# A two-block transformer kernel on one core: the first mixer's projections on rows that are not yet normed

## The reference

```
n = rmsnorm(h, g_mix)            # h * rsqrt(mean(h*h) + 1e-6) * g_mix
proj = n @ w_in                  # queries, 3 pairs of keys and values, gates, and 3 inputs of a convolution
y_conv = short_conv_mixer(b_gate, c_gate, h_conv, conv_w, w_conv_out)   # (b_gate * conv(c_gate * h_conv)) @ w_conv_out
k_cmp = compress(k_c, cmp_pos_k, w1, w2)   # blocks of 32 rows + position, then gelu(blk @ w1) @ w2; the same for v_cmp
o_all = nsa_attention(q, k_cmp, v_cmp, k_s, v_s, k_w, v_w)
mix = sigmoid(g_conv) * y_conv + sigmoid(g_attn) * (gated sum of o_all) @ w_attn_out
h = h + mix @ w_o
```

## Time and profile before

| | |
|---|---|
| time, median of 3 runs | 747.07 us (746.95 to 748.43) |
| the profiled execution's own time | 746.89 us |
| its span, first to last instruction | 745.2 us |
| PE busy | 740.4 us (99%) |
| weight loads on PE busy | 641.4 us (86%) |
| DVE busy | 518.0 us (70%) |
| ACT busy | 416.4 us (56%) |
| POOL busy | 66.5 us (9%) |
| DMA queue of SP: share of the 16 engines | 52.6% |

### The profile page before, as it was taken

One profiled execution on the slowest core, in us unless ns is written; L12 is line 12 of the kernel. 1 busy time (PEld: TensorE's weight loads), 2 busy tenths in 40 slices (PEclk: granted clock), 3 DMA queues, 4 the chain that ended last, 5 costly groups with the idle time before them and its releaser, 6 DMA issues.

```text
span 745.2 us, 11582 instructions
## 1 busy us (share of the span) xinstructions
PE 740.4 (99%) x4563; PEld 641.4 (86%) x4563; DVE 518.0 (70%) x834; ACT 416.4 (56%) x788; POOL 66.5 (9%) x103
## 2 busy tenths in 40 slices
PE   9999999999999999999999999999999999999998
PEld 8999999877888888888888888887888888888886
DVE  5784677885756678887367757898667777447762
ACT  5575557556463455565356546597646656345640
POOL 6300000000010000430000004400100000000000
PEclk9999999999999999999999999999999999999999
DMA  8998444343455546766656461735355655656611
GB/s 266 297 311 274 85 109 153 114 128 123 146 170 197 167 152 222 198 213 228 188 172 212 171 226 54 251 124 174 111 168 170 191 204 174 222 170 188 207 57 56
DMA packets 99209, 131.26 MB, mean 176 GB/s; under 512 B 5357, under 2 KB 79163, under 8 KB 99156
## 3 DMA queue, kind: packets, MB, share of 16 engines
q1 hardware_dynamic: 96564, 125.58, 52.6%
q0 software_dynamic: 2304, 4.43, 2.7%
q10 hardware_dynamic: 288, 0.52, 0.2%
HBM read 128.68 MB, written 1.84 MB: 175 GB/s over the span
## 4 chain that ended last, share of the span: by engine, by line
PE 97%; DVE 2%; ACT 1%; issue 0%; POOL 0%; POOLq 0%
PE B L1626 39%; PE B L1592 22%; PE B L1597 11%; PE B L1581 11%; PE B L1805 2%; PE B L1852 2%; PE B L1815 2%; PE B L1639 1%; PE B L1685 1%; PE B L1633 1%; DVE LO L1002 1%; PE B L1808 1%; PE B L1832 1%; PE B L1730 1%; PE B L1791 0%; PE B L1729 0%
## 5 line engine op out<-in xcount | busy, mean ns | idle before, releaser
L1002 DVE TENSOR_TENSOR LO<-RAW,HI 128x1024 fp32r<-128x1024 f32 x236 | 282.5, 1236 | 101.0 <-ACT HI L538 100.5
L1626 PE MATMUL B<-HI,AA 128*128 128x512 f32 (+1 forms) x960 | 286.8, 376 | 0.3 <-DVE AA L1008 0.2
L538 ACT ACTIVATE HI<-RAW 128x1024 fp32r<-128x1024 f32 (+1 forms) x240 | 237.2, 1038 | 63.1 <-PE B L1626 58.2
L1626 PEld LDWEIGHTS B<-HI,AA 128*128 128x128 f32 x960 | 175.7, 188 | 33.8 <-issue 1.6
L1592 PE MATMUL B<-AA,HI 128*128 128x512 f32 x704 | 179.2, 393 | 0.0
L1626 PE MATMUL B<-LO,AA 128*128 128x512 f32 (+1 forms) x480 | 178.6, 372 | 0.0
L1592 PEld LDWEIGHTS B<-AA,HI 128*128 128x128 f32 x704 | 126.8, 189 | 23.0 <-issue 0.7
L1626 PEld LDWEIGHTS B<-LO,AA 128*128 128x128 f32 x480 | 90.6, 189 | 14.6
L1597 PEld LDWEIGHTS B<-AA,LO 128*128 128x128 f32 x704 | 96.6, 190 | 7.1
L1597 PE MATMUL B<-AA,LO 128*128 128x256 f32 x704 | 98.8, 282 | 0.0
L1581 PE MATMUL B<-AA,HI 128*128 128x256 f32 x448 | 83.3, 287 | 0.0
(11 more groups left out here) (313 smaller groups left out, 634.9 us busy)
## 6 DMA issues: line engine op xcount, KB each, us to landing
RAW<-in_w_in SPq DMA_DIRECT2D x29, 1024.0 KB, 5.8
RAW<-in_w_gate SPq DMA_DIRECT2D x22, 1024.0 KB, 5.3
RAW<-in_w_up SPq DMA_DIRECT2D x22, 1024.0 KB, 5.3
RAW<-in_w_down SPq DMA_DIRECT2D x22, 1024.0 KB, 5.0
RAW<-in_w_in SPq DMA_DIRECT2D x10, 512.0 KB, 6.4
RAW<-in_w_attn_out SPq DMA_DIRECT2D x4, 1024.0 KB, 5.1
RAW<-in_w_o SPq DMA_DIRECT2D x4, 1024.0 KB, 5.0
RAW<-in_w_out SPq DMA_DIRECT2D x4, 1024.0 KB, 5.0
```

The lines of the kernel that those rows point to most:

```text
L538: e.activation(pieces(HI, NSPL, i, k), pieces(RAW, NRAW, i, k), ACT.Copy).then_inc(split_hi, 1)
L1002: e.tensor_tensor(pieces(LO, NSPL, i, k), pieces(RAW, NRAW, i, k), pieces(HI, NSPL, i, k), ALU.subtract).then_inc(split_lo, 1)
L1626: x = e.matmul(dst, a, w[:, t, c0:c0 + n], start=(first and t == 0 and k == 0), stop=(last and t == nk - 1 and k == 2))
```

## The change

The rows of x are turned as they land, with neither the norm's weights nor its factor. g_mix is loaded as 8 rows of 128, turned to one column for each group of 128 features (G8), and applied by DVE on the way out of PSUM into XT; ACT makes AH from XT, and DVE AL. The sums of squares follow later in the lists of ACT and DVE. The factor of each row is applied to what the first mixer's products give: over tokens on the free axis by a multiplication with RR (the factors spread over all partitions by a matmul with diagonals), over tokens on the partitions as a scale of the ACT instruction that reads the bank. The positions are no longer added to the blocks: they are two further columns (60 and 61, high part and rest) of the compression's stationary operand, and a new matrix SUMS1 adds them in the turn. The places of `root(1)` and of the loads into VR in POOL's list, and the weights' order, are not touched.

```diff
 SyncE
-                    e.dma_start(GAIN[0:128:64, :], A["g_mix"][0, :].rearrange("(a n) -> a n", a=2)).then_inc(row_in, 16)
+                    e.dma_start(GAIN, A["g_mix"][0, :].rearrange("(a n) -> a n", a=8)).then_inc(row_in, 16)
 GpSimd
             for kv in range(2):
                 e.memset(BLOCKS[kv][:, :, 0, 60:64].bitcast(F32), 0.0).then_inc(pads, 1)
+            e.memset(SUMS1, 1.0).then_inc(pads, 1)
+            for i, (base, sign) in enumerate(((-60, 1), (61, -1))):
+                e.wait_ge(pads, 5 + i)
+                e.affine_select(out=SUMS1, in_=SUMS1, compare_op=ALU.is_ge, fill=0.0, base=base, pattern=[[0, 64]],
+                                channel_multiplier=sign).then_inc(pads, 1)
+            e.wait_ge(pads, 7)
+            e.tensor_tensor(SUMS1, SUMS1, SUMS[:, :], ALU.add).then_inc(pads, 1)
...
             e.wait_ge(setup, FAR)
+            e.wait_ge(spread_sb, 1)
+            e.wait_ge(turn_lo, 4)
+            e.tensor_tensor(RR2, RR[:, :], RR[:, :], ALU.mult).then_inc(setup, 1)
+            def keys(br, c):
+                e.wait_ge(keys_act, 2 * br + c + 1)
+                e.tensor_tensor(KT[:, br, c, :], KT[:, br, c, :], RR[:, :], ALU.mult).then_inc(keys_sb, 1)
+            for c in range(2):
+                keys(0, c)
...
             e.wait_ge(setup, HMASK)
+            for u in range(4):
+                for k in range(2):
+                    e.wait_ge(q_act, 2 * u + k + 1)
+                    q = QT[:, u // 2, 2 * (u % 2) + k, :]
+                    e.tensor_tensor(q, q, RR[:, :], ALU.mult).then_inc(q_sb, 1)
             e.wait_ge(rel_sb, 1)
...
+            for c in range(2):
+                keys(1, c)
+            e.wait_ge(setup, SQUARED)
+            for i in range(2):
+                for c in range(2):
+                    e.wait_ge(cg_act, 2 * i + c + 1)
+                    e.tensor_tensor(CG[:, c, :], CG[:, c, :], RR2, ALU.mult).then_inc(cg_sb, 1)
+                for c in range(2):
+                    e.wait_ge(up_sb, 4 * i + 2 * c + 2)
+                    e.tensor_tensor(CG[:, c, :], CG[:, c, :], RR[:, :], ALU.mult).then_inc(cg_sb, 1)
 ScalarE
-            for t, h in ((0, 0), (1, 0), (0, 1)):
-                e.wait_ge(x_in[2 * t + h], 16)
-                squares(2 * t, X[:, t, :], QK[:, t, :], h)
+            def first_squares(h):
+                for t in range(2):
+                    e.wait_ge(x_in[2 * t + h], 16)
+                    squares(2 * t, X[:, t, :], QK[:, t, :], h)
+            def first_turned(n):
+                c, d = slice(4 * (n // 2), 4 * (n // 2) + 4), slice(128 * (n % 2), 128 * (n % 2) + 128)
+                e.wait_ge(scaled_sb, n + 1)
+                e.activation(AH[:, c, d], XT[:, c, d], ACT.Copy).then_inc(turn_hi, 1)
+            first_squares(0)
+            first_turned(0)
+            first_turned(1)
             hi(0, 0)
-            e.wait_ge(root_sb, 1)
...
+            first_turned(2)
+            first_turned(3)
             hi(0, 1)
-            for t in range(2):
-                turned(2 + t, B[5 + t], 4, t)
+            first_squares(1)
+            def spread(n):
+                e.wait_ge(spread_pe, n)
+                e.activation(RR[:, :], B[7][:, 0:S], ACT.Copy).then_inc(spread_sb, 1)
             hi(1)
+            spread(1)
+            e.wait_ge(rows_sb, 1)
+            e.wait_ge(pads, 4)
+            for kv in range(2):
+                e.activation(BLOCKS[kv][:, :, 0, 60], VT[:, 12 + 16 * kv:28 + 16 * kv], ACT.Copy).then_inc(block_hi, 1)
             def keys(br, c):
                 e.wait_ge(keys_pe, 2 * br + c + 1)
-                e.activation(KT[:, br, c, :], B[c][:, 0:S], ACT.Copy).then_inc(keys_sb, 1)
+                e.activation(KT[:, br, c, :], B[c][:, 0:S], ACT.Copy).then_inc(keys_act, 1)
...
             keys(0, 0)
 VectorE
             e.wait_ge(gain_pe, 1)
+            e.tensor_copy(G8, B[2][:, 0:8]).then_inc(half_sb, 1)
...
+            def gained(n):
+                c, d = first(n)
+                e.wait_ge(turn_pe, n + 1)
+                e.tensor_tensor(XT[:, c, d], B[5 + n % 2][:, :].rearrange("p (c q) -> p c q", c=4),
+                                G8[:, c].unsqueeze(2).to_broadcast([128, 4, 128]), ALU.mult).then_inc(scaled_sb, 1)
+            def first_low(n):
+                c, d = first(n)
+                e.wait_ge(turn_hi, n + 1)
+                e.tensor_tensor(AL[:, c, d], XT[:, c, d], AH[:, c, d], ALU.subtract).then_inc(turn_lo, 1)
...
+            gained(0)
+            gained(1)
+            first_low(0)
+            first_low(1)
+            lo(0, 0)
+            gained(2)
+            gained(3)
+            first_low(2)
+            first_low(3)
+            lo(0, 1)
             e.wait_ge(squares_sb, 4)
             e.scalar_tensor_tensor(ST[:, 4:6], ST[:, 0:4:2], EPS, ST[:, 1:4:2], ALU.add, ALU.add).then_inc(mean_sb, 1)
...
+            lo(1, 0)
+            e.wait_ge(setup, IDENT)
             e.wait_ge(root_sb, 1)
...
+            diagonals(ST[:, 6:8])
+            e.tensor_scalar(ST[:, 14:16], ST[:, 6:8], 0.5, None, ALU.mult).then_inc(half_sb, 1)
+            lo(1, 1)
             e.wait_ge(rows_pe, 1)
             e.tensor_copy(VT[:, 0:51], B[5][:, 0:51]).then_inc(rows_sb, 1)
...
             block_sums(0, SGC, 0)
+            for kv in range(2):
+                e.wait_ge(block_hi, kv + 1)
+                e.tensor_tensor(BLOCKS[kv][:, :, 0, 61], VT[:, 12 + 16 * kv:28 + 16 * kv], BLOCKS[kv][:, :, 0, 60],
+                                ALU.subtract).then_inc(block_lo, 1)
 TensorE
-            idle(14)
+            idle(12)
+            e.wait_ge(setup, IDENT)
             e.wait_ge(row_in, 16)
-            for h in range(2):
-                take(2 + h, scaled_sb, 4)
-                x = e.matmul(B[2 + h][:, :], ones[64 * h:64 * h + 1, :], GAIN[64 * h:64 * h + 1, :], start=True, stop=True)
-            x.then_inc(gain_pe, 1)
-            idle(13)
-            e.wait_ge(setup, IDENT)
+            take(2, half_sb, 1)
+            e.transpose(B[2][:, 0:8], GAIN, ident[0:8, 0:8]).then_inc(gain_pe, 1)
             def turns(h):
...
+                for t in range(2):
+                    e.wait_ge(x_in[2 * t + h], 16)
+                    take(5 + t, scaled_sb, 2 * h + t + 1)
+                    for j in range(4):
+                        o = 512 * h + 128 * j
+                        x = e.transpose(B[5 + t][:, 128 * j:128 * j + 128], X[:, t, o:o + 128], ident[:, :])
+                    x.then_inc(turn_pe, 1)
...
                     turns(0)
-                    idle(3)
+                    idle(10)
...
+            spread(1, 7)
             e.wait_ge(rows_in, 192)
             take(5, rows_sb, 1)
```

More of the change, by code:

```diff
@@ L138, in program @@
         GO = TOK[:, :, 512:768]
-        GAIN = TMP[:, 0, :]
+        GAIN = TMP[0:8, 0, 0:128]
+        RR2 = TOK[:, 0, 0:256]
+        XT = flatten(TOK[:, :, :]).rearrange("p (c n) -> p c n", c=8)
+        G8 = SM[:, 0, 0:8]
+        SUMS1 = CST[:, 0:64]
         BAND0 = GB[:, 1, :].rearrange("p (g n) -> p g n", g=4)
@@ L689, in gates @@
                                 e.wait_ge(gate_pe, 8 * n + 4 * h + t + 3)
-                                e.activation(dst[:, t, halves(h)], B[t][:, :], ACT.Tanh, scale=0.5).then_inc(gate_tanh, 1)
+                                e.activation(dst[:, t, halves(h)], B[t][:, :], ACT.Tanh,
+                                             scale=ST[:, 14 + t:15 + t]).then_inc(gate_tanh, 1)
                             yield
@@ L872, in _ @@
             hi(U_TWO + 4)
-            spread(2)
+            spread(3)
             hi(U_TWO + 5)
@@ L1036, in _, with diagonals @@
+            def diagonals(col):
+                for t in range(2):
+                    e.tensor_scalar(PT[:, 0, 128 * t:128 * t + 128], ident[:, :], col[:, t:t + 1], None,
+                                    ALU.mult).then_inc(diag_sb, 1)
+            gained(0)
[8 more added lines that the diff above has]
+            lo(0, 1)
             e.wait_ge(squares_sb, 4)
@@ L1200, in fill @@
                             own.wait()
-                            own.step(e.scalar_tensor_tensor(CG[:, c, :], UP[:, c, k:k + 256], VT[:, 4 * k + n:4 * k + n + 1],
-                                                            CG[:, c, :], ALU.mult, ALU.add))
+                            x = e.scalar_tensor_tensor(CG[:, c, :], UP[:, c, k:k + 256], VT[:, 4 * k + n:4 * k + n + 1],
+                                                       CG[:, c, :], ALU.mult, ALU.add)
+                            if k == 1:
+                                own.step(x)
+                        x.then_inc(up_sb, 1)
                         yield
@@ L1205, in fill @@
                         n = 2 * i + c
-                        own.wait()
+                        e.wait_ge(cg_sb, 4 * i + 2 + c + 1)
                         e.wait_ge(bg_pe, n + 1)
@@ L1304, in last_pair @@
                             turned(n + 2 * h + t, B[5 + t], 4 * h, t)
-            def diagonals(col):
```

(43 more changed lines are left out.)

103 lines of the change are left out of this document (41 added, 62 removed).

## The result

The changed kernel takes **757.26 us**, the median of 4 runs (756.76 to 760.73), against 747.01 for the kernel before in the runs beside it: ratio 1.0146, 95% interval 1.0111 to 1.018. It is slower by 10.25 us. The profiled execution took 757.69 us with a span of 756.0, 10.8 us more than the 745.2 before.

The account below looks back on a forecast made before the run. PE, holding 97% of the chain, was taken to bound the kernel. A block start 6.65 us later plus 2.0 us for the clock, the rest at nothing, made 8.65 us on 746.89: 755.5 us, range 751.8 to 758.4.

Parts of the forecast that it names:

- The start's gain: PE's first matmuls: first product at 10.5 instead of 12.83; after a 0.8 us wait for hi(0,1), 1.6 us won.
- The wait behind which the loads stand: POOL's root(1) gets its sum 7.3 us later, VR's loads land at 25.3, PE stands still from 19.7: the largest term.
- The chain behind the rows: From VR's turn at 25.3 through DVE's and ACT's copies to the blocks at 26.7, their start 6.65 us later.
- The clock: Block products after PE's pause run at the slow pace: 2.0 us, bounds nothing and 2.3 us.
- Rival B: VR's loads late, but PE's pace stays after the pause: 753.5 us; chance 0.22.
- The rest at nothing: Block sums, subtractions, gate tanh, SUMS1, weight loads and POOL's multiplications after the start: no cost to PE.
- a slow landing: Upper end of the range: VR's last load takes 5.9 us to land, +1.2 us.
- E: Late loads and slow pace, plus POOL's multiplications holding DVE in the attention loop, 2.6 us: 758.1 us; chance 0.10.
- C: VR's rows are there in time and only the chain to the blocks costs: +1.0, 747.9 us; chance 0.04.
- D: Faster: last VR row lands before 18.3, key copy not held by VT, blocks 1.6 us earlier: 745.3 us; chance 0.04.

Follow-up runs that it names:

- e7: Changed kernel with e10 and e2 together, and half 1's squares on ACT, their sum and the diagonals on DVE made earlier: 749.81 us, ratio 1.0039.
- e9: e7 plus e5's copy, POOL's multiplications of first keys and queries held until the seventh query copy, factors halved behind lo(1): 746.18 us, ratio 0.9986.
- e1: Changed kernel with POOL's seven loads into VR moved ahead of root(1): 753.59 us, ratio 1.0088.
- e3: Kernel before the change with POOL's seven loads into VR moved ahead of root(1): 746.69 us, ratio 0.9996.
- e10: Changed kernel with root(1) on POOL behind the seven loads and also behind the memsets and SUMS1: 751.69 us, ratio 1.006.
- e4: Changed kernel with 21 filler calls on PE between the spread and the wait for VR's loads: 756.61 us, ratio 1.013.
- e5: Changed kernel with the factors RR copied by ACT into contiguous rows, which the block sums read instead of RR with strides: 755.97 us, ratio 1.012.
- e6: Changed kernel without POOL's eight multiplications of the queries, whose row factor is left out: 757.75 us, ratio 1.0144.
- e2: e1, and ACT copies both keys before it waits for the rows and writes the position columns: 752.77 us, ratio 1.0075.

## Why the prediction was right, and where a term was off

**The start's gain.** Forecast: first product at 10.5, measured 10.08; the waits for hi(0,1), 0.8 forecast, 0.64 measured. It came a little sooner because unit 0 had landed sooner (its high part started at 8.97 instead of 9.37). e7 to e9 show that the gain is real, which the changed kernel alone could not; about 1.5 us of the forecast 1.6 are there.

**The wait behind which the loads stand.** Right in cause and size. Forecast: sum at 16.65, issues from 17.5 to 20.55, landed at 25.3, a gap of 5 to 6 us. Measured: sum at 16.1, issues from 16.93 to 19.84, landed at 24.8, gap 5.61. e1 shows the cause by taking it away, e3 that the same order was harmless before. What I had not seen is that the list held a second thing that others wait for: I had compared the BLOCKS memset with the late rows only and wrote "in time", which it was at 22.8 against 25.5; it becomes the bound the moment the loads are moved (e1, e10).

**The chain behind the rows.** Forecast from the turn to the blocks 1.4 us, measured 1.27. The start of the blocks moved by 6.07 us, forecast 6.65; the difference is within the chance of the start.

**The clock.** Forecast 2.0 us, measured 1.36 (e4 confirms it as the clock's), between the bounds; behind the same pause the blocks of e5 and e6 lost 1.8 and 1.9 us, so the price differs by the execution. The slow pace lasted 2.9 us, where the forecast had 4. The rule of the Trainium skill (TensorE: Matmul & The Clock Gate, section "HAM oscillation — how this bites in real kernels") was right in kind: the first block products behind the wait for the load ran at a granted clock of 0.50. Rival B is out. I had also written that the granted clock column does not tell the paces apart. For the start that is so; after the pause it does, with the 0.58 in the window from 25 to 30 us.

**"The rest at nothing" is the term that failed.** I wrote that the block sums "have the same four instructions of the same shape" and gave them no cost. They cost 0.57 instead of 0.41 us each, 16 x 0.168 = 2.7 us on DVE in a stage where DVE had almost no slack: it is busy 9.85 of the 10 us from 40 to 50 and 9.99 of those from 50 to 60. The shape was the same, the stride of the operand was not, and no row that I chose showed it. Taking the stride away gives back 2.04 us between the gates and the scores (e5), taking POOL's multiplications of the queries away 0.96 (e6); together that is the +2.86 us, within 0.14. So the sum 8.65 is made of 6.65 + 2.0 + 0, and the measured 10.8 of 6.07 + 1.36 + 2.86 + 0.5; two terms a little too large hid part of one that was missing. The measured 757.26 lies between 751.8 and 758.4, but the room above 755.5 had been left for a slow landing, for the clock and for E, not for the block sums. That it was enough is luck.

**Rivals.** E had the right mechanism, POOL's multiplications holding DVE, but its larger part in the wrong place: in the query stage, where I had seen only the distance to the scores, it cost about 1 us (e6). The Trainium skill's rule (SBUF — State Buffer, section "Who interferes with whom"), by which a DVE instruction with two inputs in SBUF and a GpSimd one that reads SBUF lock each other out, agrees with e6's durations: the subtractions have two such inputs. In the attention loop E cost 0.5 us instead of 2.6. Timelines of DVE in the kernel before, and of POOL and DVE in the changed one:

```profile
134.07 0.16 DVE L1150 TENSOR_SCALAR SM<-SM 128x2 f32<-128x2 f32 x1
```

```profile
143.38 1.64 POOL L499 TENSOR_TENSOR CG<-CG,RR 128x256 f32<-128x256 f32 x1 [9.12 <-DVE CG L1275]
```

```profile
144.35 0.69 DVE L1224 TENSOR_SCALAR SM<-SM 128x2 f32<-128x2 f32 x1
```

L1150 and L1224 are the same instruction. POOL's multiplication, 0.73 us alone, starts beside a subtraction of DVE that ends at 144.4, and DVE's small instruction ends together with it at 145.0: each stood for the other. DVE stays 0.5 us late, and PE waits 0.50 us for CG at 152.45. That this wait comes from there is read off the timeline; no run takes this multiplication away. C and D did not come; e9 is what D wanted, and reaches 746.2, not 745.3.

## What to carry to other kernels

When a step is moved later, go through the list of every engine that waits for it, and for everything behind the wait ask who needs it: small loads that stood harmlessly behind an early sum became a 5.6 us gap of the engine that bounds the kernel, and the clock had its price on top. When one such thing is moved out of the way, look for the next in the same list (e1, e10). An operation that "stays the same" has to be compared by strides and memories of its operands too, and a second engine that takes over work is best given it where its neighbour is idle (e9).

## What was not expected of the hardware

- A DVE product of a strided PSUM operand with a strided SBUF operand (64x240, step 2 and 16 elements) took 0.57 us, with a contiguous or a broadcast SBUF operand 0.41.
- Two POOL multiplications of 128x256 beside DVE's subtractions took 3.43 us instead of 1.5, and DVE's five instructions lost 1.1 us at the same time: together 3.0 us were lost by overlapping 1.5 us of work.
- A pause of PE of 2.4 us, with 0.8 us of idling and 0.9 us of work before it, brought the granted clock down (e1), while pauses of 1.5 us and less left it at 1.00 (e2, 1.25 us at 27.7 and 1.48 at 37.4). It fell only after PE had begun again at 21.52: 1.00 until 22.0, 0.68 in the next half microsecond, then 0.50 until 25.5.
- The same matmuls of the filler at the start of a kernel took 4.29 to 5.49 us from execution to execution, and the blocks behind the same 5.6 us pause 12.98 to 13.51 us.
